# Prompt attention with stationary values and two heads in lockstep, in a hybrid decoder step

## The reference

```python
o_lat = attend(q_lat, q_rope, ckv, k_rope)          # softmax((q.k) * SM_SCALE), causal, over a 128-wide latent
y_mla = jnp.einsum('bshr,rhv->bshv', o_lat, w_uv)   # 64 values per head
y = jnp.concatenate([y_mla, y_rw], axis=-1) @ w_out # 512 + 512 features -> 1024
```

## Time and profile before

| | us |
|---|---|
| median of 3 runs | 2544.83 (2541.89 to 2551.33) |
| the profiled execution | 2536.84 |
| its span, first to last instruction | 2535.2 |
| busy PE, DVE, ACT, POOL | 2445.7, 1395.0, 962.7, 266.9 |
| mean granted clock of PE | 0.987 |

### The profile page before, as it was taken

The page is one execution under the profiler, slowest core; times in us unless marked ns, Lnnn a source line. Parts: engine busy times, 40 slices in busy tenths (PEclk is TensorE's granted clock), DMA queues, the critical chain, the costliest instruction groups (busy, mean ns, idle before and its releaser), DMA issues.

```text
span 2535.2 us, 52352 instructions
## 1 busy us (share of the span) xinstructions
PE 2445.7 (96%) x21424; PEld 2150.3 (85%) x21424; DVE 1395.0 (55%) x2536; ACT 962.7 (38%) x1682; POOL 266.9 (11%) x309
## 2 busy tenths in 40 slices
PE   8999999999999999999998999998999999999997
PEld 7999999988777788766756998886999999998776
DVE  6555555645435656767633455554756565564623
ACT  5333333434214746533322333433433333343411
POOL 3000000000103211000000032334200000000102
PEclk8999999999999999999999999999999999999999
DMA  4222222555406444522113021245122222274441
GB/s 138 85 69 85 69 86 85 166 191 179 138 34 194 116 120 114 144 60 65 37 39 131 26 74 64 83 170 178 58 83 74 81 77 78 96 237 157 142 136 38
DMA packets 263290, 265.79 MB, mean 105 GB/s; under 512 B 35697, under 2 KB 199618, under 8 KB 261522
## 3 DMA queue, kind: packets, MB, share of 16 engines
q1 hardware_dynamic: 218738, 223.40, 27.8%
q10 hardware_dynamic: 43104, 36.31, 4.4%
q0 software_dynamic: 1216, 2.80, 0.4%
HBM read 203.88 MB, written 58.04 MB: 103 GB/s over the span
## 4 chain that ended last, share of the span: by engine, by line
PE 87%; DVE 3%; issue 3%; ACT 3%; SPq 2%; DMA 1%; POOL 1%; ACTq 0%; POOLq 0%; DVEq 0%
PE ps_b L522 18%; PE ps_a L522 18%; PE ps_b L532 11%; PE ps_a L532 11%; PE ps_rk L2691 6%; PE ps_pj L1170 4%; PE ps_wo L3485 4%; PE ps_mp L1881 2%; PE ps_mp L1907 2%; PE ps_pj L1152 1%; PE ps_mp L1895 1%; PE ps_rk L2781 1%; PE ps_mp L1866 1%; PE ps_rk L2687 1%; PE ps_rk L2833 1%
## 5 line engine op out<-in xcount | busy, mean ns | idle before, releaser
L522 PE MATMUL ps_b<-X_b,W_b 128*128 128x272 f32 x3696 | 464.8, 289 | 4.1 <-DVE X_b L722 4.1
L522 PEld LDWEIGHTS ps_b<-X_b,W_b 128*128 128x128 f32 x3696 | 464.6, 189 | 4.4 <-DVE X_b L722 4.4
L522 PE MATMUL ps_a<-X_a,W_a 128*128 128x272 f32 x3696 | 463.8, 288 | 1.8 <-issue 0.8
L522 PEld LDWEIGHTS ps_a<-X_a,W_a 128*128 128x128 f32 x3696 | 463.2, 188 | 2.4 <-issue 1.4
L532 PE MATMUL ps_b<-W_b,X_b 128*128 128x512 f32 (+1 forms) x1188 | 270.8, 390 | 0.0
L532 PE MATMUL ps_a<-W_a,X_a 128*128 128x512 f32 (+1 forms) x1188 | 270.8, 390 | 0.0
L532 PEld LDWEIGHTS ps_b<-W_b,X_b 128*128 128x128 f32 (+1 forms) x1188 | 215.9, 182 | 54.5
L532 PEld LDWEIGHTS ps_a<-W_a,X_a 128*128 128x128 f32 (+1 forms) x1188 | 215.9, 182 | 54.5
L587 ACT ACTIVATE W_a<-wraw_a 128x512 fp32r<-128x512 f32 x154 | 96.6, 628 | 224.7 <-PE ps_a L532 125.5
L587 ACT ACTIVATE W_b<-wraw_b 128x512 fp32r<-128x512 f32 x154 | 96.4, 627 | 224.4 <-PE ps_b L532 125.3
L763 DVE TENSOR_TENSOR W_b<-wraw_b,W_b 128x512 fp32r<-128x512 f32 x154 | 110.1, 716 | 114.7 <-ACT W_b L587 114.5
(11 more groups left out here) (439 smaller groups left out, 3847.4 us busy)
## 6 DMA issues: line engine op xcount, KB each, us to landing
wraw_a<-in_ffa_w_down SPq DMA_DIRECT2D x44, 512.0 KB, 3.9
wraw_b<-in_ffb_w_down SPq DMA_DIRECT2D x44, 512.0 KB, 4.2
wraw_pj<-in_w_in SPq DMA_DIRECT2D x28, 512.0 KB, 3.8
wraw_a<-in_ffa_w_gate SPq DMA_DIRECT2D x22, 512.0 KB, 4.6
wraw_a<-in_ffa_w_up SPq DMA_DIRECT2D x22, 512.0 KB, 4.6
hidden<-G_a ACTq DMA_DIRECT2D x22, 512.0 KB, 3.2
wraw_b<-in_ffb_w_gate SPq DMA_DIRECT2D x22, 512.0 KB, 4.6
wraw_b<-in_ffb_w_up SPq DMA_DIRECT2D x22, 512.0 KB, 4.6
```

The costliest lines, as they stand in the source:

```text
L522: last = nc.tensor.matmul(ps[:, bank + p, :PIECE], W[:, n % WC, wp, k * P:(k + 1) * P], operand(i, xp)[:, k, p * PIECE:(p + 1) * PIECE], s ...
```

## The change

- The products of the output (`pv`) have 64 columns of V stationary and the turned probabilities moving, two heads side by side in the two halves of PE's columns; the output is by feature. The inverse row sums are spread over 64 columns by one reciprocal for both heads, then turned by two more products; ACT copies that scale, DVE multiplies.
- The units of two heads alternate: G is 16 p + 2 i + par. PE's queue has pv ahead of the turn of the next even unit. Pieces go by half: queries and keys of head 0 and head 1 for positions 0 to 511 come first, in the V products. No sequencer loop is left.
- Keys' rotary rows come by 12 transfers of 512 columns, into three segments; weights of the next pair have buffers of their own. Some semaphores are merged: DVE's first rotation waits for all 15 transfers, SP waits for all seven constants of the sample attention.
- The output is stored by feature to `yT`, 512 columns at a time. The output projection reads prompt tiles from it and turns only the four blocks of the recurrence; the next load of rows waits for the low part (`ylo`) instead of the turn.
- In the sample attention the last two samples' pages are issued before the wait for `ql_done`. In the recurrence POOL waits for its constants ahead of two memsets.

```diff
-        wv, wq, wk = first.wv, first.wq, first.wk
+        wv, wq, wk = first.wv, (first.wq, sb("wq", [P, 2, 2, P])), (first.wk, sb("wk", [P, 2, HD]))
...
+                        for g, c in ((0, 0), (1, 0), (2, 512)):
+                            sp.dma_start(kT[row:row + ROPE, par, g, :], lat[:ROPE, 3, c:c + 512]).then_inc(consts_in.h, 16)
             before.last_stores(sp)
             first.load(sp, 1, 1)
+            load_weights(1)
             inputs.load_constants(sp)
             late.wait(sp)
-            for h in range(H - 2):
-                sp.wait_ge(pc_done.h, pc_done.at(h * NPC + NPC))
-                first.load(sp, h + 2, h % 2)
-                inputs.load_pages(sp, h)
+            for m in range(H - 2):
+                sp.wait_ge(pc_done.h, pc_done.at(8 + 4 * m))
+                if m in (0, 2):
+                    load_weights(2 + m // 2)
+                inputs.load_pages(sp, m)
...
+            def pv(N):
+                p, i = N // NTP, N % NTP
+                s = N % 2
+                pe.wait_ge(pt_dve.h, pt_dve.at(2 * N + 2))
+                if i >= 4:
+                    pe.wait_ge(pt_act.h, pt_act.at(8 * p + 2 * (i - 4) + 2))
+                pe.wait_ge(rl_made.h, rl_made.at(N + 1))
+                if N >= 2:
+                    pe.wait_ge(y_made.h, y_made.at(N - 1))
+                for par in range(2):
+                    nc.tensor.matmul(ps[head(par), 6, 256 + P * s:256 + P * s + P], rl[:, s, par, :], S.ident[:], start=True, stop=True,
+                                     tile_position=(0, HD * par), skip_group_check=True)
+                for j in range(i + 1):
+                    for par in range(2):
+                        last = nc.tensor.matmul(ps[head(par), 6, P * s:P * s + P], V[:, j, (2 * p + par) * HD:(2 * p + par + 1) * HD],
+                                                PT[:, par, j, :], start=(j == 0), stop=(j == i), tile_position=(0, HD * par),
+                                                skip_group_check=True)
+                last.then_inc(o_done.h, 1)
...
+            scores(0)
+            for G in range(NU):
+                if G + 1 < NU:
+                    scores(G + 1)
+                n = piece_at(G)
+                if n is not None:
+                    piece(n)
+                if G % 2 == 0 and G >= 2:
+                    pv(G // 2 - 1)
+                turn(G)
+            pv(NSTEP - 1)
...
+            def inverse(N):
+                dve.wait_ge(p_made.h, p_made.at(2 * N + 2))
+                if N >= 2:
+                    dve.wait_ge(o_done.h, o_done.at(N - 1))
+                nc.vector.reciprocal(rl[:, N % 2], l[:, N % 4, :].rearrange("p (a v) -> p a v", v=1).to_broadcast([P, 2, HD])).then_inc(
+                    rl_made.h, 1)
...
                 if t == 1:
-                    dve.wait_ge(consts_in.h, consts_in.at(48))
+                    dve.wait_ge(consts_in.h, consts_in.at(16 * 15))
...
+            for G in range(NU):
+                if G + 1 < NU:
+                    maxima(G + 1)
+                n = piece_at(G)
+                if n is not None and n % 2 == 0:
+                    rope(n)
+                if G % 2 == 1:
+                    inverse(G // 2)
+                pt(G)
+                if G % 2 == 0 and G >= 2:
+                    out(G // 2 - 1)
+            out(NSTEP - 1)
...
+            for b in range(H - 2, NB):
+                I.load_pages(sp, b)
             sp.wait_ge(ql_done.h, ql_done.at(1))
...
-            for b in range(H - 2, NB):
-                I.load_pages(sp, b)
...
-                    sp.wait_ge(R["y_turned"].h, R["y_turned"].at(t - 1))
+                    sp.wait_ge(R["ylo"].h, R["ylo"].at(t - 1))
...
-                for k in range(KD):
+                for k in range(KD // 2 if t < NTP else 0, KD):
                     last = nc.tensor.transpose(ps[:, turn_bank(t) + k // 4, (k % 4) * P:(k % 4) * P + r],
```

More of the change, by code:

```diff
@@ L1816, in mla_prompt, with unit, piece_of, piece_at @@
         t_done, pt_dve, pt_act, o_done, y_made = sem("t_done"), sem("pt_dve"), sem("pt_act"), sem("o_done"), sem("y_made")
+        rl_made, scale_made = sem("rl_made"), sem("scale_made")
         y_out = S.attn_out
[L1818 to L1832, removed]
+        NU, NSTEP = 2 * NTP * NQP, NTP * NQP
+        def unit(G):
+            return G // 16, G % 16 // 2, G % 2
+        def piece_of(n):
+            return n // 8, n % 8 // 4, n % 4 // 2, n % 2
+        def piece_at(G):
+            p, k = G // 16, G % 16
+            n = 8 * p + 4 + k
+            return n if k < 8 and n < 8 * NQP else None
+        def segment(p, half):
+            return 2 if half else p % 2
+        def head(par):
+            return slice(HD * par, HD * par + HD)
+        def cols(i):
+            return slice(i % 4 * P, i % 4 * P + P)
+        def unit_scores(par):
+            return ps[:, 2 * par:2 * par + 2, :].rearrange("p a b -> p (a b)")
         @blk.sync
@@ L1919, in _ @@
                 if t % 2 == 1:
-                    piece(0, 0, t // 2)
+                    piece(t // 2)
             pe.wait_ge(v_act.h, v_act.at(NTP // 2))
             pe.wait_ge(v_dve.h, v_dve.at(NTP // 2))
[L1923 to L1940, removed]
@@ L1941, in _ @@
-            heads(pe, body)
-            pv(H - 1, NTP - 1)
+            pe.wait_ge(consts_in.h, consts_in.at(16 * 15))
+            scores(0)
[9 more added lines that the diff above has]
+            pv(NSTEP - 1)
         @blk.scalar
         def _(act):
[L1946 to L1952, removed]
@@ L1954, in exps, with copy_piece @@
-            def exps(h, i):
-                G, s = h * NTP + i, i % 2
+            def copy_piece(n):
+                p, half, par, keys = piece_of(n)
+                act.wait_ge(pc_done.h, pc_done.at(n + 1))
+                if n % 4 == 0 and p >= 1:
+                    act.wait_ge(s_done.h, s_done.at(16 * p - (0 if half else 16)))
+                out = (kT if keys else qT)[:HD, par, segment(p, half), :]
+                nc.scalar.activation(out, ps[:HD, 7, :], ACT.Copy).then_inc(pc_copied.h, 1)
```

304 lines of the change are left out of this document (152 added, 152 removed).

## The result

| | us |
|---|---|
| before, median of 10 runs | 2546.68 (2541.89 to 2552.72) |
| after, median of 10 runs | 2556.49 (2553.46 to 2562.60) |
| after / before | 1.0042, 95% interval 1.0032 to 1.0052 |
| the profiled execution after, its span | 2559.84, 2557.7 |
| forecast, range | 2552.8, 2530 to 2568 |

The account below looks back on a forecast made before the run. PE was taken as the bound, busy 96% of the span. Attention +3, start +11.5, last pages -3 and output projection -3.5 made +8: 2544.8 us for the profiled execution, 2552.8 for the median, range 2530 to 2568.

Parts of the forecast that it names:

- Output product: Attention on PE: 0.055 us a record with values stationary; 30.5 us saved, 7.0 added by turns, net -23.5 of work.
- Inverse sums: Attention on DVE: one reciprocal of 128 elements a partition takes 0.97 us, bounds 0.30 and 3.2.
- The first rival: Attention: the inverse is cheap, 0.3 us, so -11 us and 2542; chance 0.13.
- The serial cycle: Attention: PE's product, turn, scores, then DVE's maxima, inverse, copy run in series; 53.1 us a pair, attention +3.
- The last pair: Attention's last two heads: missing next projections, formerly worth 5.1 us, now save only some 2.3.
- The start: Start of prompt attention: rotary transfers and head 1's weights delay first scores to 1071, +11.5 us, bounds +7 and +14.
- Last pages: Sample attention: last pages issued 11 us sooner, PE's 3.01 us wait gone, -3 us.
- Output projection: Eight tiles drop four of eight turns each: -3.5 us, 0.44 a tile, bounds -4 and 0.
- The unrolled loop: Attention's heads without sequencer loop, with merged semaphores and POOL's moved wait: 0 us, bounds -1 and +2.
- Rival 2: Attention: PE keeps its own pace, attention -30 us, total -25, 2520; chance 0.14.
- Rival 3: Attention: PE's idling makes its clock fall; seven dips add +10 to +8, 2563; chance 0.23.

Follow-up runs that it names:

- e4: Changed kernel with the reciprocal taken of two numbers a partition and spread by a copy; 2550.31 us, 1.0009 of the kernel before.
- e5: Changed kernel with DVE's inverse behind its copy of the turned block, and PE's turning of the inverse behind the output products; 2544.76 us, 0.9992 of before.
- e1: Changed kernel with DVE's first rotation waiting for its tables only, the rotary rows waited for later by PE; 2558.12 us, 1.0042 of before.
- e6: Changed kernel with the last pages issued after the latent queries and all eight turns in the output projection again; 2567.83 us, 1.0076 of before.
- b1: Kernel before with the loop over heads 2 to 5 written out, nothing else changed; 2548.80 us, 1.0012 of before (0.9998 to 1.0027).
- e8: e7 with ACT making the second head's exponentials at eight blocks ahead of its copy; 2523.33 us, 0.9902 of before.
- e3: Changed kernel with the edits of e1 and e2, and four of the 12 rotary transfers issued behind the weights; 2542.88 us, 0.9982 of before.
- e2: Changed kernel with head 1's weights issued with head 0's, before the attention; 2553.10 us, 1.0026 of before.
- e7: Changed kernel with the edits of e3, e4 and e5 in one; 2528.18 us, 0.9925 of before.

## Why the prediction was right, point by point

- **Output product: right by the record, too large by the stage.** 0.055 a record, as in the earlier trace rows. But over the attention PE's busy time fell from 200.9 to 186.2 us, 14.7 less where the forecast had 23.5 of work less. About 5 of the difference is shown: the group at 1208.63 takes 1.46 us to the next turn, 0.15 more than the 1.31 of the forecast, in 32 steps. The rest is open. The forecast was spared this error, as PE's work did not set the pace.
- **Inverse sums: right.** 0.952 forecast as 0.97. The first rival is wrong in its condition. Its price was too high as well: e4 gave 6.2 us where it had 11.
- **The serial cycle: right in kind, a little long.** Forecast 7.3, 8.0 and 7.7 for six, seven and eight blocks; the cycles that start at 1208.63, 1215.60 and 1223.24 take 6.97, 7.64 and 7.74. At four and five blocks they take 5.63 and 6.29 where 6.1 and 6.7 stood; at one to three, 6.48, 5.34 and 6.20 where 6.0, 5.4 and 5.9 stood. A pair came to 52.28 instead of 53.1. The last pair took 4.1 us less than that, not 2.3, while the last two heads before took 46.67, 6.2 less than two of 26.45 and not 5.1. Together the attention came to -0.4 instead of +3. e5 shows the mechanism by itself: the same work in another order, 2.64 us a pair less. The gain of PE's work did turn into waits: 21.6 us of them, where the attention before had 7.7.
- **The start: right.** +11.9 against +11.5. Rotary rows and weights ended as worked out. The first part of PE's wait turned out not to count by itself (e1), and a dip to 1.2 GHz, which the term did not have, is in it with 1.5 us.
- **Last pages: right,** -4.2 against -3; the issue moved 11.05 us against 11. The 1.2 more is the clock: over this stage PE was busy 92.4 us in the kernel before, with the dip of the earlier trace rows, and 91.1 after. The second profile of the kernel before had no such extra (91.1) and a wait of 4.6. In e6 the stage gives back 5.1: the wait shown is 3.8, and PE was busy 92.3 us, 1.2 more than after.
- **Output projection: right by the tile,** 0.44 less in each; but the stage is only 1.7 shorter than before and 2.9 shorter than in e6. PE has a new wait of 1.1 on the low part in the first tiles. e6, with all turns back, has the same 1.1, so the missing turns don't make it; whether the split in two instructions, the later loads of rows or DVE's queue does was not tested. The other 0.7 is open.
- **The unrolled loop: the step with the doubt.** Taken as 0 with bounds of -1 and +2; b1 puts it at +3 (-1 to +7), the middle above the upper bound; its cause is likely the straight program and not shown.
- **Rival 2 (PE keeps its own pace): wrong** for this order of the queues, and its price was too high. In e8 PE waits in the attention for less than before (6.4 us against 7.7), and yet a pair takes 48.87 where the rival had 45.4, and the attention 15.9 us less than before where it had 30: PE's busy time there is 185.5 us, 15 less than before and not 23.5 or more.
- **Rival 3 (the clock falls): wrong in size, its mechanism is there.** The attention after has a granted clock of 1.00 from its first scores to its end, though PE is idle for 2.3 of the 26 us shown. But the last stretch of the attention, between the last two stores, has 0.89 in e3 and 0.94 in e2, e4, e5, e6 and e7; only after, e1 and e8 have 1.00 there. It took 29.97, 29.04 and 29.12 us in e3, e2 and e6, where after and e1 took 27.46 and 27.47 with the same attention: one dip of 1.6 to 2.5 us at the end, not seven. The windows view of e3 and the last output product of e3 and of after:

```profile
1242.50:1272.50 30.00, 24.74 (x189) 17.30 (x189) 17.84 (x33) 10.59 (x23) 0.57 (x2) 0.89 0.06 18
```

```profile
1267.81 3.63 PE L1942 MATMUL ps_mp<-PT_mp,V_mp 128*64 128x128 f32 x32
```

```profile
1279.72 1.92 PE L1939 MATMUL ps_mp<-PT_mp,V_mp 128*64 128x128 f32 x32
```

  The profiled execution of after had no such dip. Whether its other runs had one is not known, and it is a candidate for a part of what stays open below.

With what was measured the sum is +11.9 - 0.4 - 4.2 - 3.5 + 1.1 = +4.9, and +7.9 with b1's middle value, against 8 to 13 by the interval. So the forecast of +8 had errors that cancel: the attention 3.4 too high, and the pages 1.2; the output projection and the unrolled loop some 4 too low. Start and serial cycle are shown; that the total came within 2 us of the measured one is in part luck. Some 2 us between the sum and the medians stay open; b1's interval alone is wider.

## What to carry to other kernels

Shortening an engine's work pays only if no serial cycle through another engine closes at the same time: write down the order of both queues, and put what is needed last (here a reciprocal) behind what is needed first. Waits in a row at a start hide each other, so count the end of the last one and not their lengths, and try them out together before one of them is called harmless. A single profiled execution can differ from another of the same program by 10 us in a stage that nobody touched; compare stages, and take a second profile before a difference outside the change is explained.

## What the runs showed of the hardware

The reciprocal's slope between one and eight elements holds to 128. The rows of after and of e4 by form have 952 ns at 128x128 and 165 at 128x2, 6.2 ns an element:

```profile
L2059 DVE RECIPROCAL rl_mp<-l_mp 128x128 f32<-128x128 f32 x32 | 30.5, 952 | 1.2 <-ACT Pb_mp L1990 0.8
```

The repeat count of 8 that the Trainium skill gives for it ("VectorE: DVE Perf Modes", "First, the fixed hardware budget") was an estimate of 1.2 us in the prediction. The measurement decides: 0.95 us, which at the 0.96 GHz of that estimate is nearer to six cycles an element. A copy of the same shape took 227 ns, so a reciprocal that is to be spread takes 165 + 227 = 392 ns if it is made on the few elements first, and 952 if not.

PE's clock fell to 1.2 GHz at the start of the attention, after PE had been idle for 6.3 us (after, e2) or 11.0 (e1: the four records took 3.69 us). In the attention itself it fell late: in six of the nine kernels of the change (e2 to e7) the last output product, behind waits of 1.78 and 0.78 us with one turn between them, took 3.2 to 3.6 us where it took 1.92 in after and e1, and the stretch around it has a granted clock of 0.89 to 0.94. In after and e1 PE had the same waits, 21.6 us in sum and none above 1.8, and the granted clock stayed at 1.00. So the length of the waits alone does not tell whether it falls.
